# Two of four modulation blocks go from row sums on VectorE to strips on TensorE, and two gate pieces are loaded earlier

## The reference

```python
mod = silu(c) @ ada_w + ada_b             # 1024 -> 6 * 1024
sh1, sc1, gt1, sh2, sc2, gt2 = split(mod, 6)
h = rms_norm(x, norm1_g) * (1 + sc1) + sh1
proj = h @ w_in                           # q, k, v, g, gk, z, xbc, dt, gates
o_a = gla_mixer(...)                      # linear attention
o_b = ssd_mixer(...)                      # state space mixer, causal convolution over xbc
x = x + gt1 * ((gate_a * (o_a @ w_oa) + gate_b * (o_b @ w_ob)) @ w_out)
h = rms_norm(x, norm2_g) * (1 + sc2) + sh2
x = x + gt2 * hier_moe(h, ...)            # 32 experts, two a token, all expert weights are read
return rms_norm(x, final_norm_g)
```

## Time and profile before

| | us |
|---|---|
| median of three runs | 700.7 |
| the profiled execution | 700.86 |
| its span, first to last instruction | 699.0 |
| TensorE busy | 669.4 (96%) |
| VectorE busy | 420.1 (60%) |
| ScalarE busy | 264.8 (38%) |
| data moved | 201.23 MB, 288 GB/s over the span |

### The profile page before, as it was taken

One profiled execution on the slowest core, in us unless ns is written; L12 is line 12 of the kernel. 1 busy time (PEld: TensorE's weight loads), 2 busy tenths in 40 slices (PEclk: granted clock), 3 DMA queues, 4 the chain that ended last, 5 costly groups with the idle time before them and its releaser, 6 DMA issues.

```text
span 699.0 us, 12784 instructions
## 1 busy us (share of the span) xinstructions
PE 669.4 (96%) x5402; PEld 538.5 (77%) x5402; DVE 420.1 (60%) x710; ACT 264.8 (38%) x373; POOL 71.4 (10%) x70
## 2 busy tenths in 40 slices
PE   8999999999999999999998999899999999999893
PEld 8999999998777777999988997675666666665441
DVE  4656788987866789977786678644333122221226
ACT  3346545557763624335552332312131121221003
POOL 0001000000003614300000000001112111111111
PEclk9999999999999999999999999999999999999998
DMA  8987764455343443346639976999999999999992
GB/s 363 423 353 243 298 248 175 130 177 191 121 157 130 161 142 121 122 140 253 241 108 397 410 280 249 423 421 418 419 397 418 421 421 421 419 418 418 420 355 95
DMA packets 31195, 201.23 MB, mean 288 GB/s; under 512 B 5047, under 2 KB 5431, under 8 KB 7970
## 3 DMA queue, kind: packets, MB, share of 16 engines
q1 hardware_dynamic: 27378, 193.27, 70.7%
q0 software_dynamic: 3760, 7.14, 2.8%
HBM read 195.35 MB, written 10.75 MB: 295 GB/s over the span
## 4 chain that ended last, share of the span: by engine, by line
PE 77%; DVE 9%; DMA 6%; ACT 3%; issue 2%; SPq 2%; DVEq 0%; POOL 0%; ACTq 0%; POOLq 0%
PE ps L1571 75%; DMA ring<-in_expert_pieces 4%; DVE ring_rounded L934 2%; DMA ring<-in_pieces 2%; ACT ring_rounded L644 2%; SPq L461 1%; PE ps L1988 1%; PE ps L1692 1%; DVE r_ct L1209 1%; DVE r_v L1209 1%; DVE r_xs_rounded L1239 1%; ACT sq L760 1%; DVE g_sb L1142 0%; DVE r_kq L1173 0%; DVE newton L920 0%
## 5 line engine op out<-in xcount | busy, mean ns | idle before, releaser
L934 DVE TENSOR_TENSOR ring_rounded<-ring,ring_rounded 128x2048 fp32r<-128x2048 f32 x60 | 136.8, 2291 | 38.8 <-ACT ring_rounded L644 38.5
L1571 PE MATMUL ps<-hT_rounded,ring_rounded 128*128 128x256 f32 x832 | 150.1, 286 | 1.1 <-ACT hT_rounded L658 1.1
L1571 PEld LDWEIGHTS ps<-hT_rounded,ring_rounded 128*128 128x128 f32 x832 | 129.2, 193 | 5.1 <-issue 3.9
L644 ACT CAST ring_rounded<-ring 128x2048 fp32r<-128x2048 f32 x60 | 114.1, 1906 | 34.4 <-PE ps L1571 18.8
L1571 PE MATMUL ps<-ring_rounded,hT_rounded 128*128 128x512 f32 x352 | 109.7, 393 | 0.9 <-DVE ring_rounded L934 0.9
L1571 PE MATMUL ps<-x_sb_rounded,ring_rounded 128*128 128x256 f32 x416 | 109.8, 284 | 0.0
L1571 PEld LDWEIGHTS ps<-x_sb_rounded,ring_rounded 128*128 128x128 f32 x416 | 77.3, 193 | 0.9 <-issue 0.2
L1571 PEld LDWEIGHTS ps<-ring_rounded,hT_rounded 128*128 128x128 f32 x352 | 64.3, 188 | 14.8 <-issue 1.4
L858 ACT ACTIVATE sq<-ps 128x128 f32<-128x128 f32 x32 | 8.9, 277 | 142.6 <-PE ps L1571 142.6
L1454 DVE TENSOR_TENSOR r_st<-ps,r_kq 128x512 f32<-128x512 f32 x32 | 22.1, 692 | 65.0 <-PE ps L1571 65.0
L603 POOL DMA_INDIRECT y_rows<-r_st,r_btm x29 | 28.5, 984 | 311.4 <-DVE r_st L1454 298.6
(11 more groups left out here) (336 smaller groups left out, 1002.9 us busy)
## 6 DMA issues: line engine op xcount, KB each, us to landing
ring<-in_pieces SPq DMA_DIRECT2D x66, 1024.0 KB, 5.0
ring<-in_expert_pieces SPq DMA_DIRECT2D x48, 1024.0 KB, 17.5
r_z<-in_expert_pieces SPq DMA_DIRECT2D x12, 1024.0 KB, 13.3
r_xs<-in_expert_pieces SPq DMA_DIRECT2D x12, 1024.0 KB, 12.5
r_v<-in_pieces SPq DMA_DIRECT2D x6, 1024.0 KB, 7.2
r_ct<-in_pieces SPq DMA_DIRECT2D x6, 1024.0 KB, 5.6
g_sb<-in_expert_pieces SPq DMA_DIRECT2D x6, 1024.0 KB, 17.2
r_st<-in_expert_pieces SPq DMA_DIRECT2D x6, 1024.0 KB, 17.9
```

Source lines behind the costliest of these rows:

```text
L644: nc.scalar.copy(high_of(p_), slot_of(p_)).then_inc(hi_ok, 1)
L934: nc.vector.tensor_tensor(low_of(p_), slot_of(p_), high_of(p_).bitcast(F32), ALU.subtract).then_inc(lo_ok, 1)
L1571: return nc.tensor.matmul(o, l, r, start=start, stop=stop)
```

## The change

Blocks 8 and 9 become strips on TensorE, behind convolution units 3 and 4, with their four pieces in the ring. Only blocks 6 and 7 stay row sums. Gate pieces 0 and 1 are issued where block 8's row pieces were, once block 7 has been summed. The bias is added to eight columns of `mod` instead of 16, since `modulation_out` adds it for blocks 8 and 9.

```diff
-ADA_AFTER = {("xbc", i): 3 + i for i in range(1, 3)}
+ADA_AFTER = {("xbc", i): (4, 5, 8, 9)[i - 1] for i in range(1, 5)}
 QUARTERS = KD // 2
-ADA_ORDER = [("quarter", q) for q in range(QUARTERS)] + [("ada", i) for i in range(4, 6)]
+ADA_ORDER = [("quarter", q) for q in range(QUARTERS)] + [("ada", i) for i in ADA_AFTER.values()]
...
-ROW_PIECES = [("row", i, h, 0) for i in range(6, 10) for h in range(2)]
-ROWS_AT = {("oa", 1, 1): 7, ("ob", 0, 1): 8, ("ob", 1, 1): 9}
+ROW_PIECES = [("row", i, h, 0) for i in range(6, 8) for h in range(2)]
+ROWS_AT = {("oa", 1, 1): 7}
...
-                if n >= LOADS and PIECES[n - LOADS] in (("ob", 0, 0, 1), ("ob", 1, 0, 1)):
+                if n >= LOADS and PIECES[n - LOADS] == ("ob", 0, 0, 1):
                     piece_used(sp, PIECES[n - LOADS])
-                    load_rows(8 + PIECES[n - LOADS][1])
+                    sp.wait_ge(start_row_read, 4 + len(ROW_PIECES))
+                    for p_q in GATE_ROWS[:2]:
+                        sp.dma_start(slot_of(p_q), piece_src(p_q)).then_inc(s_gate, 16)
                 load_piece(n, p_)
...
             load_moe(4)
             load_moe(5)
-            sp.wait_ge(start_row_read, 4 + len(ROW_PIECES))
-            for p_ in GATE_ROWS[:2]:
-                sp.dma_start(slot_of(p_), piece_src(p_)).then_inc(s_gate, 16)
             for p_ in GATE_ROWS[2:]:
                 load_piece(PIECE_AT[p_], p_)
...
                         if (name, i, h) in ROWS_AT:
-                            if (name, i) == ("ob", 1):
-                                before((("out", 0), 0))
+                            split_to(SPLIT_AT["ob", 0, 0, 1] + 1)
                             rows_out(ROWS_AT[name, i, h])
             dve.wait_ge(start_row_read, 4 + len(ROW_PIECES))
-            link(nc.vector.tensor_tensor(mod[:, 24:40], mod[:, 24:40], col("ada_b", 24, 16), ALU.add))
+            link(nc.vector.tensor_tensor(mod[:, 24:32], mod[:, 24:32], col("ada_b", 24, 8), ALU.add))
```

## The result

| | before | after |
|---|---|---|
| median of the runs compared, us | 699.7 (698.32 to 700.85, 4 runs) | 706.51 (705.71 to 707.56, 4 runs) |
| ratio, 95% interval | | 1.0101 [1.0082, 1.012] |
| profiled execution, us | 700.86, span 699.0 | 706.41, span 704.6 |
| mean granted clock | 0.991 | 0.984 |

The change makes the kernel slower, by 6.8 us in the medians and 5.55 in the profiled executions. The forecast was +2.9 and 703.6, its range ended at 706.0.

What follows compares the result with a forecast made beforehand. Bounds: TensorE's work before the experts, when expert transfers start and how full the 16 slots are. +4.16 + 2.07 + 2.0 - 2.39 - 2.9 = +2.9 us gave 703.8 profiled, 703.6 as forecast; range 699.5 to 706.0.

Steps and rivals of the forecast that it cites:

- the bank wait: Before the 32 narrow products: "small" moves from bank 6 to 4 and waits for ACT's q copy, +2.07 us.
- the strips: Behind convolution units 3 and 4: blocks 8 and 9 cost TensorE 2.08 us each, +4.16 us on the path.
- the sums: Before the output projection's second residual add: without DVE's row sums TensorE's idle there goes, -2.39 us.
- no wait for a ring piece: Convolution units 3 and 4: four more ring pieces cost nothing; a late piece would be up to 1 us.
- The queue term: In front of the experts: a shorter transfer queue lands piece 16 in 4.9 us instead of 7.8, lead kept, -2.9 us.
- the head start gives nothing: Rival on expert transfers: a queue run nearly empty may not keep 420 GB/s, 2.9 comes back, 706.5 us; chance 8%.
- The clock term: At the narrow products: after the idle the clock falls at about 61.3 and the products left take twice as long, +2.0 us.
- the 4.07 of the sum: At the narrow products: the bank wait of 2.07 us and the clock's 2.0 us together.
- it stays: Third quarter of `ob` 0: the 3.2 us stall for a ring piece keeps its whole queue and remains, 0 us change.
- the prediction's 4.5 and 3.3: Piece 16: by the skill's fixed cost an empty queue would take 4.5 us, the queue term 3.3; measured 4.9 preferred.

Runs made afterwards that it cites:

- E1: The changed kernel with one line more, the narrow projection "small" keeping bank 6 as before the change; 701.15 us, ratio 1.002 to the kernel before.
- E8: The changed kernel with nine unread products filling the wait before "small" and the `ob` 0 ring piece loaded ahead of the expert rows; 699.71 us, ratio 1.0004.
- E2: The kernel before with only "small" moved to bank 4, behind half 0 of q; 704.53 us, ratio 1.0069.
- E6: The kernel before with only the `ob` 0 ring piece's load issued earlier, by two SP lines; 697.31 us, ratio 0.9973.
- E4: The changed kernel with gate pieces 0 and 1 issued at their old place, behind expert pieces 4 and 5; 706.29 us, ratio 1.0093 to the kernel before.
- E7: The changed kernel without blocks 8 and 9, neither strips nor sums, their values the bias alone; 695.74 us, ratio 0.9956 to the kernel before.
- E3: The changed kernel, bank 4 kept, with nine unread products run while TensorE waits before "small"; 700.07 us, ratio 1.0003 to the kernel before.
- E5: The changed kernel with "small" in bank 6 and the `ob` 0 ring piece loaded ahead of rows 7, experts 0 and 1 and gate bias; 696.79 us, ratio 0.9961.

## Why the prediction was wrong

Its direction held, and most of its steps did: the bank wait (forecast 2.07, measured 2.04, released by ACT's q copy), the strips (4.16; 4.26), the sums (-2.39; -2.64), no wait for a ring piece in the units with new strips. The size failed: 706.5 us against 703.6, 2.9 over. In the profiled executions (706.41 against the sum's 703.8) 2.6 of them are found, and 2.5 of those in one step, the queue term, if the tail is counted with it:

**The queue term, the step that failed.** The prediction had -2.9, "the lead is kept". The first half was right: piece 16 was issued at 470.54 and landed 4.8 us later, where it had taken 7.8. The lead was not kept. The rival "the head start gives nothing" had named a reason, a queue run nearly empty that doesn't keep 420 GB/s, and its figure, 706.5, is what was measured; it had 8%, and the range stopped short of it. The 20 us from the issue of piece 16, before and then after, all engines:

```profile
464.51:484.51 20.00, 20.00 (x186) 13.29 (x184) 5.29 (x19) 3.79 (x9) 2.04 (x2) 1.00 1.01 418
```

```profile
470.54:490.54 20.00, 20.00 (x186) 13.29 (x184) 5.29 (x19) 3.78 (x9) 2.04 (x2) 1.00 0.92 343
```

TensorE did the same work in both, and SP's issues in these 20 us stand at the same distances from piece 16's. DMA moved 8.35 MB before and 6.85 after, 1.5 MB or some 3.6 us of transfer less. Piece by piece, as time since the issue of piece 16, pieces 16 to 19 landed 2.95, 1.83, 1.83 and 1.87 us sooner than before, and piece 20 0.27 later. The whole lead was spent within five pieces. The later windows of the changed kernel:

```profile
474.00:478.00 4.00, 4.00 (x56) 3.03 (x53) 0.36 (x2) 0.88 (x3) 0.00 (x0) 1.00 0.99 383
478.00:482.00 4.00, 4.00 (x30) 2.27 (x30) 1.48 (x6) 1.02 (x2) 0.00 (x0) 1.00 0.99 379
482.00:486.00 4.00, 4.00 (x42) 2.86 (x39) 0.61 (x3) 0.68 (x2) 1.03 (x1) 1.00 0.92 330
486.00:490.00 4.00, 4.00 (x34) 2.27 (x32) 2.32 (x8) 0.61 (x2) 1.00 (x1) 1.00 0.93 370
490.00:494.00 4.00, 2.68 (x29) 1.99 (x25) 3.47 (x10) 1.30 (x3) 0.01 (x1) 1.00 1.01 425
```

From 474 to 490 that is 4 x (37 + 41 + 90 + 50) = 872 KB less than at 420 GB/s, 2.1 us of transfer, with two to four pieces issued and not landed; before there were three to four throughout. By 490 the pieces took 8.9 us from issue to landing again, as in the kernel before (8.8). The share of 0.99 in windows of 380 GB/s says that engines busy with a packet are not engines at full rate.

What holds instead is simpler: from the issue of piece 16 to the last wait it took 197.75 us before, 196.46 after, and in E1 to E8 196.84, 197.81, 198.28, 197.69, 197.11, 197.64, 196.85 and 198.61. The three with a full queue (before, E2, E6) lie within 0.2 us of each other, the seven with the emptier one 1.3 below to 0.9 above them. So the -1.29 of the table is one profile's figure, and the head start gives nothing that can be told from its scatter of 2.2 us. To that accuracy a microsecond in front of the experts reaches the end whole: their start lay anywhere from 459.6 to 470.5.

**The clock term, placed right, priced once.** The +2.0 stood on one profiled execution, which had one slow stretch already. In the changed kernel's profile it came to 3.89 - 2.04 = 1.85, and once the clock had fallen the narrow products did take twice as long, which the prediction assumed with no row to show it. Over many runs the bank is dearer, 4.6 (E2) to 5.4 (E1) against the 4.07 of the sum, since kernels without the wait mostly have no slow stretch here: of five profiles only that of the kernel before has one. That the +2.0 fitted the profiles so well is in part luck.

**A stretch that was not in the sum.** The prediction said of `ob` 0 "it stays". The wait did, with 2.86, but the slow stretch behind it grew from one full window at 0.50 to two (1.7 us of missing clock before, 3.4 after), net +0.52 with what is smaller elsewhere. That its length is not fixed, the rows of before could not show: E1 has 3.4 there, E2, E4 and E7 1.7, E3, E5, E6 and E8 nothing. By the clock of all runs the sum's +2.0 for the clock should have been some +3.4 to +3.8.

**The tail, +0.9, was not in the sum.** TensorE's last products now wait 0.51 for DVE, and DVE, one step before, for row transfers:

```profile
687.75 1.28 DVE L1520 SCALAR_TENSOR_TENSOR x_sb<-r_z,r_btm,x_sb 128x1024 f32<-128x1024 f32 x1 [0.17 <-DMA r_z<-y_rows]
689.49 1.28 DVE L1520 SCALAR_TENSOR_TENSOR x_sb<-r_z,r_btm,x_sb 128x1024 f32<-128x1024 f32 x1 [0.46 <-DMA r_z<-y_rows]
```

From the last expert wait to the end it is 37.6 us here, 37.7 in E1 and E5, but 36.7 to 36.9 before and in the other six. E3, E4 and E8 have the same strips, so these aren't the cause. The row transfers are late (their median from issue to landing is 8.5 us after and 7.1 before), and so are the last expert pieces: the last but one landed 16.9 to 17.0 us behind the last wait in the three profiles with the longer tail, and 15.4 to 16.0 in before, E2, E3 and E4. E3's expert pieces fall back by about as much, but ahead of its last wait. So tail and queue are one account: from piece 16's issue to the end of the span it is 234.5 us before and 234.1 after, -0.4 in place of -2.9, and over all ten profiles 233.6 to 235.5. What makes the pieces fall back stays open; no run was made on it.

**Where it was measured from.** The last 0.3 is the step from the profile to the median. Before's profiled 700.86 lay above what more runs gave (699.7, 699.89, 699.31), the changed kernel's 706.41 did not. That is why the medians say 6.8 where the profiles say 5.55.

**The exchange itself.** Strips for sums cost 4.1 to 4.5 and returned 2.6 to 3.6. With the bank kept (E1) the change is 0.2% slower than before, at the edge of what can be told. Most of its loss is a side effect, through a table of banks dealt from the end of a list.

## What to carry to other kernels

When names are added to a list from which buffers or banks are dealt, write down who gets which one before and after: here that cost more than the work the change moved. Price an idle gap on TensorE by more than its length, above all next to small products (the idle of 2.39 us before 438.46 had no slow stretch behind it, the 2.04 ahead of the narrow products had), and if it can't go, put products into it. Do not count a lead in a transfer queue as kept: ask what the queue's depth will be while the lead lasts. Clear a late piece ahead of it instead, which was two lines here and, with the bank kept, gave 696.79 us (0.9961 [0.9945, 0.9977]); in the kernel before the two lines alone gave 697.31.

## What the runs showed of the hardware

- One and the same wait of 2.04 us costs 4.6 to 5.4 us of run time ahead of 32 products of 48 columns. With nine products that nobody reads in its place (E3) the kernel is 6.4 us faster, part of it behind `ob` 0, and the narrow products take 3.80 us instead of 5.76.
- Slow stretches are not a property of the code alone: at 60 to 70 us the profiles show three 2 us windows at 0.50 to 0.52 with the wait (after, E2, E4), one without it (before) or none (E1, E5, E6, E7), and one with it filled (E3) or none (E8).
- With the granted clock at half, a product of 48 columns starts every 0.21 us instead of every 0.11 (after, 61.9 to 65.5 us).
- With two to four 1 MB pieces issued and not landed, DMA moved 330 to 383 GB/s with its engines 0.92 to 0.99 busy (after, 474 to 490 us); with three to four all the time it moved 418 (before). A lead of 2.95 us in the queue was gone after five pieces.
- The Trainium skill (DMA: Bandwidth & Descriptors, Anatomy of one DMA) gives a transfer issued from GpSimd a fixed cost of about 2.0 us. These pieces are issued by SP, which the prediction's 4.5 and 3.3 passed over, though its sum did not use them; the 4.8 us of a 1 MB piece in an empty queue would leave room for such a part, and no run here separates it.
